# Split weights stored with two blocks woven word by word, and loaded into TensorE with a step of two words

## The reference

```
hn = rmsnorm(h); proj = hn @ w_in + b_in                 # mLSTM, short conv, two merge gates
merged = sigmoid(gm) * (hm @ w_branch_m) + sigmoid(gc) * (yc @ w_branch_c)
h = h + merged @ w_out
u = causal_dwconv(rmsnorm(h) @ w_up) + b;  gate, val = split(u)     # d_ff = 5504
h = h + (silu(gate) * val) @ w_down;  h = rmsnorm(h)
h = h + rmsnorm(gla_mixer(rmsnorm(h)));  h = h + rmsnorm(mla_mixer(rmsnorm(h)))
```

## Time and profile before

| | |
|---|---|
| median of 3 runs | 2235.48 us |
| the profiled execution | 2237.68 us, span 2235.9 us, granted TensorE clock 0.985 |
| PE, PEld, DVE, ACT, POOL busy | 96%, 94%, 58%, 53%, 11% |
| matmuls | 17596 recorded |
| DMA | 393.83 MB, mean 176 GB/s, stream queue 48.6% busy |

### The profile page before, as it was taken

The page is one execution under the profiler, slowest core; times in us unless marked ns, Lnnn a source line. Parts: engine busy times, 40 slices in busy tenths (PEclk is TensorE's granted clock), DMA queues, the critical chain, the costliest instruction groups (busy, mean ns, idle before and its releaser), DMA issues.

```text
span 2235.9 us, 46586 instructions
## 1 busy us (share of the span) xinstructions
PE 2143.3 (96%) x17596; PEld 2097.6 (94%) x17596; DVE 1302.6 (58%) x1641; ACT 1187.9 (53%) x1565; POOL 255.9 (11%) x325
## 2 busy tenths in 40 slices
PE   5999999999999999999999999999999979999996
PEld 5999999999999999999999999899998969899996
DVE  5656565454556666666665455556665465756544
ACT  5454545554546656666665444644554445655542
POOL 2000000100110000000001001000101123111112
PEclk8999999999999999999999999999999989999998
DMA  3545545555555455454555555454545434444453
GB/s 149 188 170 181 176 177 198 188 191 203 187 189 188 173 183 188 169 188 169 188 179 202 220 207 196 162 181 177 181 163 180 171 132 142 160 150 152 150 185 113
DMA packets 54927, 393.83 MB, mean 176 GB/s; under 512 B 6097, under 2 KB 6225, under 8 KB 7522
## 3 DMA queue, kind: packets, MB, share of 16 engines
q1 hardware_dynamic: 54432, 392.19, 48.6%
q10 hardware_dynamic: 450, 1.02, 0.1%
HBM read 391.09 MB, written 2.10 MB: 176 GB/s over the span
## 4 chain that ended last, share of the span: by engine, by line
PE 61%; issue 19%; DVE 9%; ACT 7%; POOL 3%; DVEq 1%; ACTq 1%; DMA 0%; POOLq 0%
PE acc L554 17%; PE acc L555 17%; PE acc L556 17%; ACT w_hi L921 4%; DVE w_lo L1326 3%; PE tok L596 2%; PE tok L598 2%; PE tok L597 2%; DVE f_pre L1551 1%; ACT L1097 1%; DVE f_val L1562 1%; DVE f_val L1558 1%; DVE f_act L1571 1%; POOL sumsq_g L1894 1%; PE att L614 1%
## 5 line engine op out<-in xcount | busy, mean ns | idle before, releaser
L1326 DVE TENSOR_TENSOR w_lo<-raw,w_hi 128x1024 fp32r<-128x1024 f32 x740 | 906.7, 1239 | 780.7 <-ACT w_hi L921 778.4
L554 PE MATMUL acc<-n_hi,w_hi 128*128 128x256 f32 x3488 | 987.5, 283 | 42.2 <-POOL n_lo L1903 20.2
L555 PE MATMUL acc<-n_lo,w_hi 128*128 128x256 f32 x3488 | 977.7, 280 | 0.0
L556 PE MATMUL acc<-n_hi,w_lo 128*128 128x256 f32 x3488 | 977.5, 280 | 0.0
L921 ACT ACTIVATE w_hi<-raw 128x1024 fp32r<-128x1024 f32 x740 | 759.7, 1053 | 389.6 <-DMA raw<-stream_in 164.6
L554 PEld LDWEIGHTS acc<-n_hi,w_hi 128*128 128x128 f32 x3488 | 665.2, 191 | 49.9 <-issue 20.2
L555 PEld LDWEIGHTS acc<-n_lo,w_hi 128*128 128x128 f32 x3488 | 662.0, 190 | 0.5
L556 PEld LDWEIGHTS acc<-n_hi,w_lo 128*128 128x128 f32 x3488 | 662.1, 190 | 0.0
L555 PE MATMUL acc<-f_lo,w_hi 128*128 128x256 f32 x688 | 193.6, 281 | 0.0
L556 PE MATMUL acc<-f_hi,w_lo 128*128 128x256 f32 x688 | 193.6, 281 | 0.0
L554 PE MATMUL acc<-f_hi,w_hi 128*128 128x256 f32 x688 | 193.6, 281 | 0.0
(11 more groups left out here) (313 smaller groups left out, 2980.2 us busy)
## 6 DMA issues: line engine op xcount, KB each, us to landing
raw<-stream_in SPq DMA_DIRECT2D x370, 1024.0 KB, 4.8
x<-x_in SPq DMA_DIRECT2D x4, 512.0 KB, 7.3
out<-x SPq DMA_DIRECT2D x4, 512.0 KB, 2.7
v_bias<-v_bias_in ACTq DMA_DIRECT2D x1, 512.0 KB, 8.9
par<-params_in ACTq DMA_DIRECT2D x1, 287.0 KB, 5.5
pos_i<-positions_in ACTq DMA_DIRECT2D x1, 128.0 KB, 6.8
gk<-gk_in ACTq DMA_DIRECT2D x1, 68.0 KB
```

Of the source, the lines that this page charges most:

```text
L554: nc.tensor.matmul(out, w_hi[:, s, wc], hi[:, k, :], start=first, stop=False)
L555: nc.tensor.matmul(out, w_hi[:, s, wc], lo[:, k, :], start=False, stop=False)
L556: return nc.tensor.matmul(out, w_lo[:, s, wc], hi[:, k, :], start=False, stop=last)
L1326: nc.vector.tensor_tensor(w_lo[:, s, :], raw[:, s, :], w_hi[:, s, :].bitcast(fp32), ALU.subtract).then_inc(lo_ready, 1)
```

## The change

In a unit of a feature-major stage, block 2q and block 2q+1 now share 256 words: word 2e is column e of the first, word 2e+1 column e of the second. ACT and DVE write `w_hi` and `w_lo` in that order (and DVE reads `w_hi` so); `raw` stays as it is. A weight load then takes its 128 words with a step of two words, over 1024 bytes instead of 512. Token-major units (4 to 7 of mix, 8 to 15 of gla, 6 and 7 of mla) keep the old layout. The number, order and waits of the instructions on each engine are the same; sizes, transfers and addresses of tensors too. In the list of instructions the two split operations of a woven unit are now written 128x4x2x128 where they were 128x1024.

```diff
+        TOKEN_UNITS = {"mix": range(4, 8), "gla": range(8, 16), "mla": range(6, 8)}
+
+        def is_woven(name, j):
+            return name not in TOKEN_UNITS or j not in TOKEN_UNITS[name]
+
+        def plain(t, s):
+            return t[:, s, :].rearrange("p (q b e) -> p q b e", b=2, e=P)
+
+        def woven(t, s):
+            return t[:, s, :].rearrange("p (q e b) -> p q b e", b=2, e=P)
...
             def tile(out, s, c, hi, lo, k, first, last):
-                wc = slice(c * P, (c + 1) * P)
-                nc.tensor.matmul(out, w_hi[:, s, wc], hi[:, k, :], start=first, stop=False)
-                nc.tensor.matmul(out, w_hi[:, s, wc], lo[:, k, :], start=False, stop=False)
-                return nc.tensor.matmul(out, w_lo[:, s, wc], hi[:, k, :], start=False, stop=last)
+                high, low = woven(w_hi, s)[:, c // 2, c % 2, :], woven(w_lo, s)[:, c // 2, c % 2, :]
+                nc.tensor.matmul(out, high, hi[:, k, :], start=first, stop=False)
+                nc.tensor.matmul(out, high, lo[:, k, :], start=False, stop=False)
+                return nc.tensor.matmul(out, low, hi[:, k, :], start=False, stop=last)
...
-                nc.scalar.activation(w_hi[:, s, :], raw[:, s, :], ACT.Copy).then_inc(hi_ready, 1)
+                nc.scalar.activation(to(w_hi, s), plain(raw, s), ACT.Copy).then_inc(hi_ready, 1)
...
-                nc.vector.tensor_tensor(w_lo[:, s, :], raw[:, s, :], w_hi[:, s, :].bitcast(fp32),
+                nc.vector.tensor_tensor(to(w_lo, s), plain(raw, s), to(w_hi, s).bitcast(fp32),
                                         ALU.subtract).then_inc(lo_ready, 1)
```

More of the change, by code:

```diff
@@ L912, in split, with high @@
                 u, s, use = unit_of(name, i, j + RING)
-                high(u, s, use)
-            def high(u, s, use):
+                high(u, s, use, woven if is_woven(name, j + RING) else plain)
+            def high(u, s, use, to=woven):
                 if s % 2 == 0:
@@ L1320, in split, with rest @@
                 u, s, _ = unit_of(name, i, j + RING)
-                rest(u, s)
-            def rest(u, s):
+                rest(u, s, woven if is_woven(name, j + RING) else plain)
+            def rest(u, s, to=woven):
                 dve.wait_ge(hi_ready, u + 1)
-                nc.vector.tensor_tensor(w_lo[:, s, :], raw[:, s, :], w_hi[:, s, :].bitcast(fp32),
+                nc.vector.tensor_tensor(to(w_lo, s), plain(raw, s), to(w_hi, s).bitcast(fp32),
                                         ALU.subtract).then_inc(lo_ready, 1)
```

## The result

| | before | after |
|---|---|---|
| median of four runs each | 2237.01 us (2233.53 to 2241.02) | 2299.34 us (2297.18 to 2302.96) |
| ratio, 95% interval | | 1.028 (1.0255 to 1.0305) |
| span of the profiled execution | 2235.9 us | 2301.2 us |
| granted clock, mean | 0.985 | 0.982 |

The change costs 62 us; the forecast was a gain of 79. The time lies outside the forecast's own range (2134 to 2185) and just inside the upper end of the range over all cases (2300), 9 us above the half case of rival 3 (2290).

The account below looks back on a forecast made before the run. TensorE bounds the kernel through the distance between matmul starts. Gains of 20.4 (lower level), 27.5 (upper) and 38.9 us (mixed stages), less 8 for chains, give 79: 2157 us, chance 0.38; own range 2134 to 2185, all cases 2135 to 2300.

Parts of the forecast that it names:

- rival 3: Feature-major matmuls: a meeting is paid per piece of memory, so the excess doubles, 2346 us; half of it 2290; chance 0.22.
- the price of a matmul: Woven feature-major matmuls: 108 ns, estimated as half of the 216 of a plain float32 matmul; before 113.3 and 117.6.
- An excess isn't inherent in loading and streaming side by side.: TensorE: a plain float32 matmul of 256 columns is within 2 ns of twice 106.7, so the excess could go.
- Two read streams in the same partition that meet: Feature-major matmuls: load and stream meet at the same memory at a fixed price, giving excesses of 6.6 and 11 ns.
- equal pace, no meeting: Woven load and stream both walk 1024 bytes, keep their distance and no longer meet repeatedly; before, they drifted 512 bytes a matmul.
- twice as many pieces of memory: Bound on the woven matmul: the load meets the stream twice as often, excess doubles to 120 and 128.5 ns.
- Rival 1: Feature-major matmuls: the load itself needs 113.3 ns, weaving only ends the upper level's extra meetings; 24 us gained, 2212; chance 0.15.
- The splits: I take no change.: ACT and DVE split operations: writing with a step of two words leaves them at 1053 and 1239 ns.
- rival 4: Split operations slow by a tenth or more; wup alone gives 30 us back, 2187 us; chance 0.08.
- Wup isn't set by TensorE.: Wup: an ACT and DVE chain sets the double iteration, which stays at 23.4 us; nothing gained there.
- Token-major stretches unchanged.: Token-major stretches of the kernel: their matmul times stay as before; listed among the signs of a right forecast.
- the covers: Outside wup nothing else becomes late: splits and the weight stream keep up; a tenth of wdown's 20 us could be lost.

Follow-up runs that it names:

- the offsets above: Kernel before, unwoven, with the streamed activations at four other distances from the weights by the remainder to 256 bytes: 2269.58, 2279.44, 2263.62 and 2266.44 us.
- the runs on the stream's walk: Kernel before with load, stream or both standing on one word, or walking with a step of two, by stage: 111.7 ns a matmul with both standing.
- the splits-only run: Changed kernel with ACT and DVE still writing units woven, but weight loads taking 128 adjacent words: 2245.04 us, ratio 1.0032.
- the run with the nudge: Kernel before with one extra matmul of 64 columns ahead of wdown and one ahead of mlaout: 2233.22 us, ratio 0.998.
- the step alone: Kernel before with feature-major weight loads taken at a step of two words, splits still written plain: 2291.29 us, ratio 1.0223.

## Why the prediction was wrong

**The law that fits the runs.** A matmul of this kernel takes the longest of three times: its load's lines, its stream's lines, each at about 1.8 ns, and a floor of 111.7 ns for 128 columns loaded. It is a fit to these runs at the offset of the kernel before; it has no term for the other offsets, nor for the loads of 64 and 96 columns beside a full stream.

| operand | lines of 16 bytes | ns a matmul | ns a line |
|---|---|---|---|
| load, adjacent (stream standing) | 32 | 111.7 | not the bound |
| load, step two (stream standing) | 64 | 117.8 | 1.84 |
| load, step three | 96 | 173.3 | 1.81 |
| load, step four | 128 | 235.6; 233.3 at half the clock | 1.84, 1.82 |
| stream, 256 adjacent (load standing: 113.3) | 64 | 113.3 / 117.8 | 1.77 / 1.84 |
| stream, 192 with step two | 96 | 173.4 | 1.81 |
| stream, 256 with step two; 512 adjacent | 128 | 229.3; 229 to 233 | 1.79 to 1.82 |

Before, the load had 32 lines and slack, and the stream's 64 set the pace. Woven, the load has 64 too, and two equal bounds running side by side come out at 120.0, 2.2 ns above the 117.8 of such a load alone and of the stream's upper level. Where those last 2.2 ns come from isn't settled. The times don't add up: with a load of 128 lines beside a stream of 64 the matmul takes 235, not 345. This agrees with the Trainium skill, "TensorE: Matmul & The Clock Gate", step-by-step section, which gives the two operands read ports of their own; the offsets above, 113.3 to 120.0 ns for the same two plain operands, suggest that they aren't wholly independent, unless it is the stream's own address that counts.

**The steps, one by one.** The step that failed is the price of a matmul, 108 ns for the woven load: the forecast took the excess over 106.7 for a meeting that equal pace would end, and it is a price by lines of 16 bytes, of which the woven load touches twice as many (120.0 measured).

- *"An excess isn't inherent in loading and streaming side by side."* This is where it went wrong. It rested on the plain float32 matmul of the earlier trace rows, whose spacing was within 2 ns of twice 106.7. But that form takes 215 ns for the same 64 lines of stream, 3.4 ns a line, so a limit of 1.8 ns a line can't show in it. I took the absence of a cost in a form that couldn't pay it as a sign that the cost could go. The floor with nothing walking is 111.7 (the runs on the stream's walk), so 108 was out of reach for any layout.
- *"Two read streams in the same partition that meet"; equal pace, no meeting.* The 512-column matmul at 233.3 was read as an excess of 20 ns over 213.3, caused by the load. It is the stream's own time, 128 lines: 229 comes out too when 256 columns are streamed with a step of two. The drift theory made equal pace a gain; what equal pace meant was twice the lines for the load. The two levels that I leaned on exist, but a stage changes its level without any change to its own instructions (wdown in the splits-only run, glaout in the run with the nudge), they are 4.4 ns apart, and neither leads to 108. What chooses the level is open.
- *The bound "twice as many pieces of memory", 120 and 128.5,* held its lower value and was in the right direction, for another reason: no price per meeting, or the upper level would have gone to 128.5. I weighed it at 0.22, below the forecast. That the time, 2299, lies near half of that rival's loss (2290) is no confirmation of it.
- *Rival 1, the load as the bound at 113.3,* had the load's own bound nearly right: it is 111.7 for an adjacent load. The 113.3 is the stream's, since it stays when the load stands on one word.
- *"The splits: I take no change."* Half right. DVE is free at a step of two (1233). ACT isn't: 1145, and 102 ns more within wup. The mechanism of rival 4 was right, its size was not: only one of the three operations of the chain grew, so wup lost 86 x 0.102 = 8.8 us (8.2 measured), against the 30 written there.
- *Wup isn't set by TensorE.* Right, and tested: with the step alone its double iteration stayed at 23.40 us at 120 ns a matmul.
- *Token-major stretches unchanged.* Right.

**The sum again,** with 120.0 for 108.0 and the same counts: lower level 3846 x 6.67 = 25.7 us, upper 2832 x 2.2 = 6.2, mixed 5187 x 4.5 = 23.3, wup 8.2: 63.4, against 65.3 between the two spans. The counts and the covers stood. Two terms failed: the price of a matmul, with its sign (55 us of the 63), and the split on ACT, put at nothing without a row that had such a step (8 us).

**The rule that was cited.** The measured steps first: a step of two in the load took it from under the 111.7 ns floor to 117.8, in ACT's write from 1053 to 1136 ns, in DVE's write and read nothing (1224); one word a line doubled all three (235.6, 2068, 2040). The Trainium skill, "SBUF — State Buffer", section "Door 1: The DMA port swizzle", has two hits on a 16-byte line as enough for the full rate. DVE agrees; the load and ACT don't, and here the measurement decides. That the price jumps at one word a line agrees.

## What to carry to other kernels

Count the lines of 16 bytes that each operand of a matmul touches, per matmul, for load and stream apart. In this kernel the larger count at about 1.8 ns a line was the price, never below 111.7 ns with 128 columns loaded, and a layout that spreads a 128-word load over twice the bytes uses up the slack that the load had. When a price is borrowed from another form of instruction because it shows no excess there, ask first whether that form reads fast enough to meet the limit. A stage set by a chain of ACT and DVE must be costed by each operation in the chain: a copy that gets 9% longer shows in full, whatever TensorE does.

## What the hardware showed that I had not expected

- The time per line isn't TensorE's: a load of 128 lines took 235.6 ns at a granted clock of 1.00 and 233.3 at 0.50.
- Fewer columns loaded isn't faster beside a full stream: 64 columns took 119.0 ns, 96 took 117.3, where 128 took 113.3 or 117.8. With a standing stream 64 took 109.2.
- A load with a step of eight took 241.1 ns and one of four 235.6, for the same number of lines.
- A matmul that streams 192 float32r columns stayed at the floor of its load (111.7 ns), and one that streams 64 beside an adjacent load brought the granted clock down to 0.50.
- Where the streamed tensor begins, by the remainder to 256 bytes, is worth up to 6.7 ns a matmul (113.3 to 120.0), and of the five pairs tried the kernel before has the best. Whether it is its distance to the weights or its own place that counts, and why, is open.
